# Modulation by column halves, later tables, and gate rows through DRAM, in a two-layer diffusion transformer block

## The reference

```python
sh1, sc1, gt1, sh2, sc2, gt2 = split(silu(cond) @ w_ada[l] + b_ada[l], 6)
h = rmsnorm(x, norm_mix_pre[l]) * (1 + sc1) + sh1
y = mixer(h)                      # w_in, four kinds of attention, w_o
x = x + gt1 * rmsnorm(y, norm_mix_post[l])
h = rmsnorm(x, norm_ffn_pre[l]) * (1 + sc2) + sh2
x = x + gt2 * rmsnorm(channel_mixer(h), norm_ffn_post[l])
```

## Time and profile before

| | us |
|---|---|
| median of three runs | 1594.75 (1592.17 to 1596.13) |
| the profiled execution | 1590.41 |
| its span on the core | 1588.2 |
| TensorE busy | 1516.3 (95%) |
| VectorE, ScalarE, GpSimd busy | 1166.0, 972.7, 116.3 |

### The profile page before, as it was taken

One profiled execution on the slowest core, in us unless ns is written; L12 is line 12 of the kernel. 1 busy time (PEld: TensorE's weight loads), 2 busy tenths in 40 slices (PEclk: granted clock), 3 DMA queues, 4 the chain that ended last, 5 costly groups with the idle time before them and its releaser, 6 DMA issues.

```text
span 1588.2 us, 22081 instructions
## 1 busy us (share of the span) xinstructions
PE 1516.3 (95%) x7825; PEld 1233.5 (78%) x7825; DVE 1166.0 (73%) x1001; ACT 972.7 (61%) x951; POOL 116.3 (7%) x167
## 2 busy tenths in 40 slices
PE   5989999999898999999999999999999999999996
PEld 2866799988676778878878887887887887887884
DVE  2568444535567548888888888888888888888886
ACT  3444444323544457777777777777777777777773
POOL 2430130000020110000000000000000000000001
PEclk9999999999998999999999999999999999999998
DMA  9966665567752379999999999999999999999991
GB/s 368 294 222 208 221 174 174 173 224 265 288 191 93 128 284 324 370 362 372 384 366 363 380 366 352 388 371 349 388 369 354 384 367 352 388 367 340 394 385 72
DMA packets 221317, 484.91 MB, mean 305 GB/s; under 512 B 8800, under 2 KB 41872, under 8 KB 221264
## 3 DMA queue, kind: packets, MB, share of 16 engines
q1 hardware_dynamic: 215024, 466.38, 81.3%
q0 software_dynamic: 6240, 17.80, 4.1%
HBM read 475.34 MB, written 8.81 MB: 305 GB/s over the span
## 4 chain that ended last, share of the span: by engine, by line
PE 89%; DVE 4%; ACT 3%; DMA 1%; issue 1%; POOL 1%; POOLq 0%; DVEq 0%; SPq 0%; ACTq 0%
PE ps L1700 23%; PE ps L1701 23%; PE ps L1705 23%; PE ps L1715 4%; PE ps L1722 3%; PE ps L1716 3%; PE ps L1745 2%; PE ps L2144 2%; DMA raw<-in_w_ada 1%; PE ps L1784 1%; PE ps L1923 1%; PE ps L1880 1%; ACT probs L851 1%; DVE sm L1283 1%; DVE qz L1247 1%
## 5 line engine op out<-in xcount | busy, mean ns | idle before, releaser
L1153 DVE TENSOR_TENSOR w_lo<-raw,w_hi 128x2048 fp32r<-128x2048 f32 (+1 forms) x397 | 905.6, 2285 | 204.1 <-ACT w_hi L771 201.5
L771 ACT ACTIVATE w_hi<-raw 128x2048 fp32r<-128x2048 f32 (+1 forms) x397 | 757.7, 1913 | 260.7 <-PE ps L1701 241.0
L1700 PE MATMUL ps<-w_hi,x_hi 128*128 128x512 f32 (+1 forms) x1216 | 436.1, 369 | 4.1 <-ACT w_hi L771 2.7
L1701 PE MATMUL ps<-w_hi,x_lo 128*128 128x512 f32 (+1 forms) x1216 | 430.9, 365 | 0.0
L1705 PE MATMUL ps<-w_lo,x_hi 128*128 128x512 f32 (+1 forms) x1216 | 285.9, 365 | 0.0
L1700 PEld LDWEIGHTS ps<-w_hi,x_hi 128*128 128x128 f32 x1216 | 229.0, 188 | 44.8 <-issue 5.2
L1701 PEld LDWEIGHTS ps<-w_hi,x_lo 128*128 128x128 f32 x1216 | 229.1, 188 | 38.0
L1705 PEld LDWEIGHTS ps<-w_lo,x_hi 128*128 128x128 f32 x1216 | 207.8, 188 | 39.9
L1700 PE MATMUL ps<-w_hi,h_hi 128*128 128x512 f32 x520 | 205.4, 395 | 4.9 <-DVE h_lo L1485 4.3
L1701 PE MATMUL ps<-w_hi,h_lo 128*128 128x512 f32 x520 | 205.4, 395 | 0.0
L1705 PE MATMUL ps<-w_lo,h_hi 128*128 128x512 f32 x520 | 139.0, 392 | 0.0
(11 more groups left out here) (265 smaller groups left out, 1074.2 us busy)
## 6 DMA issues: line engine op xcount, KB each, us to landing
raw<-in_moe_w_gate SPq DMA_DIRECT2D x112, 1024.0 KB, 6.4
raw<-in_moe_w_up SPq DMA_DIRECT2D x112, 1024.0 KB, 7.1
raw<-in_moe_w_down SPq DMA_DIRECT2D x112, 1024.0 KB, 6.7
raw<-in_w_ada SPq DMA_DIRECT2D x48, 1024.0 KB, 6.1
raw<-in_w_in SPq DMA_DIRECT2D x20, 960.0 KB, 11.0
raw<-in_ffn_w_gate SPq DMA_DIRECT2D x11, 1024.0 KB, 5.5
raw<-in_ffn_w_up SPq DMA_DIRECT2D x11, 1024.0 KB, 5.9
raw<-in_ffn_w_down SPq DMA_DIRECT2D x11, 1024.0 KB, 5.7
```

The lines of the kernel that those rows point to most:

```text
L771: act.activation(split_hi(c, slice(0, width(c))), raw[:, r % NRAW, 0:width(c)], ACT.Copy).then_inc(hi_done, 1)
L1153: dve.tensor_sub(split_lo(c, n), raw[:, raw_of(c) % NRAW, n], split_hi(c, n)).then_inc(lo_done, 1)
L1700: pe.matmul(out, xh, split_hi(c, w), start=start, stop=False, skip_group_check=True)
L1701: last = pe.matmul(out, xl, split_hi(c, w), start=False, stop=False, skip_group_check=True)
```

## The change

1. Scale and shift of layer 0 are made by column halves: units 4, 5, 0, 1 give columns 0 to 511 of both, units 6, 7, 2, 3 the rest. The stream has the first `w_in` contraction halves between them, and TensorE runs the first halves (h = 0) of blocks 0 to 2 for both sequences before the second halves. Between these first halves stand ada 6, 7 and 2, 3. The `w_in` blocks take six PSUM banks in turn instead of four. ScalarE keeps the second half of the transposes in `h` (`keep_T`).
2. The constants are reordered; the first load has 144 columns, the other 832 come by a second load ahead of the cache loads of layer 0, and these now start at the third `hi` instead of the second.
3. `gates` and `gate_rows` go. Once per layer and channel, TensorE transposes the gate columns of both sequences (`gate_cols`, two transposes), ScalarE copies them out, GpSimd stores them to DRAM (`gate_store`, 8 KB) and loads each sequence's row into all 128 partitions of `xn` (`gate_load`, 512 KB).

```diff
-            units += ada(0, 4, 5, 6, 7, 0, 1, 2, 3) + win + ada(0, 8, 9, 10, 11)
+            units += ada(0, 4, 5, 0, 1) + win[0:1] + ada(0, 6, 7) + win[2:3] + ada(0, 2, 3) + win[4:5] + win[1:6:2] + win[6:] + ada(0, 8, 9, 10, 11)
...
-ROW_BANK = {(0, 1): 7, (0, 0): 6, (1, 1): 1, (1, 0): 1}
+ROW_BANK = {(0, 1): 0, (0, 0): 0, (1, 1): 1, (1, 0): 1}
...
+def section_of(l, n):
+    if l == 0 and n < 8:
+        return (0, 1 - n // 2 % 2), 1 - n // 4, n in (4, 6), n in (1, 3)
+    return (l, n // 4), n // 2 % 2, n % 4 == 0, n % 4 == 3
...
-            return 4 * s if l or which else 2 * s
+            return 4 * s if l or which else 4 + 2 * s
...
-            src = ps[:, 2 + 2 * (j % 2) + s, :]
+            src = ps[:, 2 + 2 * (j % 3) + s, :]
...
-            pool.dma_start(cst[:, :], consts).then_inc(in_cst, 16)
+            pool.dma_start(cst[:, 0:C_FIRST], consts[:, 0:C_FIRST]).then_inc(in_cst, 16)
...
+            def gate_store(n):
+                pool.wait_ge(g_evac, n + 1)
+                pool.dma_start(g_dram[n].rearrange("s t c -> t s c"), g_cols[:, :, :]).then_inc(g_out, 16)
+                pool.wait_ge(g_out, 16 * (n + 1))
+            def gate_load(n, s):
+                if n % 2:
+                    pool.wait_ge(nT, 4 * n + 2 * s + 2)
+                else:
+                    pool.wait_ge(oT, n + s + 1)
+                pool.dma_start(xn[:, s, :], bass.AP(tensor=g_dram[n].tensor, offset=s * D, ap=[[0, P], [1, D]])).then_inc(g_in[s], 16)
...
-                    pool.wait_ge(hi_done, 2)
+                    pool.wait_ge(hi_done, 3)
+                    pool.dma_start(cst[:, C_FIRST:C_N], consts[:, C_FIRST:C_N]).then_inc(in_tables, 16)
...
+            def keep_T(s):
+                act.wait_ge(nT, 2 * s + 2)
+                act.activation(h_of(0, 0)[s][:, 512:1024], ps[:, T_bank(0, 0, s) + 1, :], ACT.Copy).then_inc(nkeep, 1)
...
+            def gate_cols(l, which, b):
+                n = 2 * l + which
+                act.wait_ge(g_T, n + 1)
+                if n:
+                    act.wait_ge(g_out, 16 * n)
+                act.activation(g_cols[:, :, :], ps[0:KT, b, 0:2 * P].rearrange("t (s c) -> t s c", s=2), ACT.Copy).then_inc(g_evac, 1)
...
                     rows(0, 1)
+                    split_to(1)
+                    for s in range(2):
+                        keep_T(s)
+                        norm_hi(0, 0, s, (0,))
+                    split_to(2)
                     rows(0, 0)
+                    split_to(4)
+                    act.wait_ge(nkeep, 2)
                     for s in range(2):
                         norm_h(0, 0, s)
-                        norm_hi(0, 0, s)
-                        split_to(s + 1)
+                        norm_hi(0, 0, s, (1,))
...
-                for n in range(2):
-                    gate_rows(l, 0, 0, n, n)
                 post_half(l, 0, 0)
...
-                dve.wait_ge(gbs, 2 * q + 2)
+                dve.wait_ge(g_in[s], 16 * (2 * l + which + 1))
...
                     section(0, 1)
...
+                        norm_h(0, 0, s)
+                        norm_lo(0, 0, s, (0,))
+                        split_to(s + 1)
+                    split_to(3)
                     section(0, 0)
+                    split_to(4)
                     for s in range(2):
+                        norm_lo(0, 0, s, (1,))
...
-            def gates(l, which, s, n, b):
+            def gate_cols(l, which, b):
                 k = 3 * which + 2
                 pe.wait_ge(mod_ready, SECTIONS.index((l, k)) + 1)
-                for i in range(4):
-                    last = pe.matmul(ps[:, b, cols(i, P)], mod[:, l, k, 4 * n + i, s:s + 1].to_broadcast([P, P]), ident(),
-                                     start=True, stop=True)
-                last.then_inc(gb, 1)
+                for s in range(2):
+                    last = pe.transpose(ps[0:KT, b, cols(s, P)], mod[:, l, k, :, s], ident())
+                last.then_inc(g_T, 1)
...
             def attention(l):
+                pe.wait_ge(win_evac[1], NWIN * l + 3)
...
+                    if i == 9:
+                        for s in range(2):
+                            pe.wait_ge(prep_evac[s], np_(s) * (l + 1))
+                        gate_cols(l, 0, 6)
                     item_out(l, i)
...
-                        if j == 0:
-                            if s:
-                                pe.wait_ge(gbs, 2 * (4 * l + 1))
-                            for n in range(2):
-                                gates(l, 0, s, n, n)
...
-                    if 1 <= f <= 4:
-                        pe.wait_ge(gbs, f + 3)
-                        gates(0, 1, (f - 1) // 2, (f - 1) % 2, 1)
+                    if f == 1:
+                        gate_cols(0, 1, 1)
...
-                for n in range(2):
-                    gates(1, 1, 0, n, 6 + n)
+                gate_cols(1, 1, 6)
...
-                pe.wait_ge(r_row, 1)
-                for n in range(2):
-                    gates(1, 1, 1, n, n)
...
+                if l == 0:
+                    for j in range(3):
+                        for s in range(2):
+                            w_in_unit(j, 0, s)
+                            for n in {(0, 1): (6, 7), (1, 0): (2, 3)}.get((j, s), ()):
+                                ada(0, n)
+                            if j == s == 1:
+                                columns(0, 0)
+                    for j in range(3):
+                        for s in range(2):
+                            w_in_unit(j, 1, s)
```

More of the change, by code:

```diff
@@ L191, in win_u, with win_c, half_count @@
     return SPLIT.index(("win", l, 0)) + 2 * j
+def win_c(l, j, h):
+    return SPLIT.index(("win", l, 2 * j + h))
+def half_count(q, h):
+    return 2 * h + q + 1 if q < 2 else 2 * q + h + 1
 def wo_u(l, j):
@@ L275, in program @@
         h_dram = nc.dram_tensor("h_rows", (2 * P, D), F32, kind="Internal").ap()
+        g_dram = [nc.dram_tensor(f"gate_rows{n}", (2, KT, P), F32, kind="Internal").ap() for n in range(2 * DEPTH)]
         y_dram = nc.dram_tensor("y_rows", (3 * P, D), F32, kind="Internal").ap()
@@ L822, in norm_h, with norm_hi @@
                     if q < 2:
-                        src, scale = h[:, P * k:P * k + P], 1.0
+                        src = h[:, P * k:P * k + P]
                     last = act.activation(h[:, P * k:P * k + P], src, ACT.Identity, bias=mod[:, l, 3 * which, k, s:s + 1], scale=scale)
                 last.then_inc(nh[1], 1)
-            def norm_hi(l, which, s):
+            def keep_T(s):
+                act.wait_ge(nT, 2 * s + 2)
+                act.activation(h_of(0, 0)[s][:, 512:1024], ps[:, T_bank(0, 0, s) + 1, :], ACT.Copy).then_inc(nkeep, 1)
+            def norm_hi(l, which, s, halves=(0, 1)):
                 q = 4 * l + 2 * which + s
-                for h in range(2):
+                for h in halves:
                     act.wait_ge(nh[h], q + 1)
@@ L1210, in norm_h, with norm_lo @@
                 last.then_inc(nh[0], 1)
-            def norm_lo(l, which, s):
+            def norm_lo(l, which, s, halves=(0, 1)):
                 q = 4 * l + 2 * which + s
-                for h in range(2):
+                for h in halves:
                     n = slice(512 * h, 512 * h + 512)
-                    dve.wait_ge(nhi, 2 * q + h + 1)
+                    dve.wait_ge(nhi, half_count(q, h))
                     dve.tensor_sub(x_lo[:, s, n], h_of(l, which)[s][:, n], x_hi[:, s, n]).then_inc(nlo, 1)
@@ L1734, in ada @@
             def ada(l, n):
-                r, h, m = AT["ada", l, n], n % 2, SECTIONS.index((l, n // 4))
-                if n % 4 == 0:
+                at, i, first, last_of = section_of(l, n)
+                r, h, m = AT["ada", l, n], n % 2, SECTIONS.index(at)
+                if first:
                     same = [i for i in range(m) if row_bank(i) == row_bank(m)]
@@ L1744, in ada @@
                 for kt in range(4):
[L1745 to L1746 removed]
+                    last = pe.matmul(row_ps(m)[CG * kt:CG * kt + CG, :], cond[:, 4 * h + kt, i, :],
+                                     raw[:, r % NRAW, 512 * kt:512 * kt + 512], start=first, stop=last_of)
                 last.then_inc(ada_used, 1)
```

128 lines of the change are left out of this document (66 added, 62 removed).

## The result

The changed kernel takes 1570.24 us in the median (1568.72 to 1572.64, four runs); the kernel before, timed beside it, 1595.44 (1592.17 to 1598.58). The ratio of the two is 0.9844, 95% interval 0.9819 to 0.9868. That is 25 us less, where 16.6 were forecast; it is 1.8 us under the low end of the range. The direction and the order of the work came as forecast. The size did not.

The account below looks back on a forecast made before the run. TensorE, with 89% of the chain of waits, was taken as the bound. Terms 4.9 + 7.3 + 3.3 + 1.1 = 16.6 us took 1590.41 to 1573.8; adding 4.3 for the timed median gave 1578, range 1572 to 1588.

Parts of the forecast that it names:

- four terms: Forecast gains: start of layer 0 4.9 us, out-projections 7.3, dense stage 3.3, before the experts 1.1; together 16.6.
- The start: Start of layer 0: four ada loads instead of eight ahead, attention's first ada at 87.2 us instead of 92.1, gain 4.9.
- the stall of a microsecond that the margins allowed: Start of layer 0: margins of 0.6 to 1 us for later operands, so a stall of about 1 us was possible.
- the 26.6: Start of layer 0: forecast time in us of the first w_in product, 10.1 us earlier than before.
- rival C: Start of layer 0 gains nothing, its halves adding hand-overs; total gain 11.7 us, 1583 us; chance 0.09.
- Gate rows: Out-projections and dense stage without gate-row products: forecast gains of 7.3 and 3.3 us.
- 9.8 us to go: Out-projections: time forecast for the gate-row load, from its issue at 157.4 us to gated() at about 167.2.
- Rival D: Out-projections: gate-row load lands late, 24 us in all, stalling each layer 14 us; about 1606 us; chance 0.05.
- Before the experts: Routing step without gate products: at most 2.3 us saved, term 1.1 us, bounds -1 and 2.3.
- The half of it that the text gave back to the clock: Before the experts: gather running wholly at half clock, giving back about 1.2 of at most 2.3 us.

Follow-up runs that it names:

- e2: The changed kernel with the constants' tile one column wider (977), so the tiles behind it lie as in the kernel before; 1579.11 us, ratio 0.9904.
- e16: The kernel before with the constants' tile at 1008 columns instead of 977; 1576.07 us.
- e9: The changed kernel with an 8-column gap ahead of its first tile, every tile 32 bytes further, distances kept; 1570.28 us, ratio 0.9855.
- e7: The changed kernel with the constants' tile at 992 columns instead of 976, everything behind it 64 bytes further; 1571.65 us.
- e3: The kernel before with the gate part of the change alone and the constants' tile at 992 columns; 1573.13 us, ratio 0.9866.
- e1: The kernel before with one edit, the constants' tile 992 columns wide instead of 977; 1584.80 us, ratio 0.9939.
- e4: The changed kernel with its gate part taken back, new start and 976-column constants' tile kept; 1581.22 us, ratio 0.9917.
- e5: The changed kernel with x_hi and x_lo (and the small tiles behind them) moved 32 bytes; 1580.13 us, ratio 0.9904.
- e15: The changed kernel with the constants' tile at 1104 columns, everything behind it 512 bytes further; 1570.95 us.
- e8: The changed kernel with 12 products nobody reads added in the routing step, where gate products were removed; 1570.74 us, ratio 0.9847.
- e14: The changed kernel with the constants' tile at 1040 columns, everything behind it 256 bytes further; 1572.31 us.
- e12: The changed kernel with the constants' tile at 1008 columns, everything behind it 128 bytes further; 1560.02 us.

## Why the prediction was wrong, point by point

**The step that failed** is the sum: "4.9 + 7.3 + 3.3 + 1.1 = 16.6 us. The profiled execution took 1590.41 us ... : 1573.8." It subtracts four terms and leaves every other product at its duration of before, a term put at nothing without a reason. The text read the new order of the constants as a matter of their transfer ("144 of 977 columns") and nowhere as a matter of where the tiles behind them lie. e2 shows the missing term: with the old distances the changed kernel takes 1579.1, 1.1 us from the forecast of 1578.0, and it is 15.4 us faster than the kernel before beside it, where 16.6 were forecast. The term that had to stand beside the four is the pace of some 6,000 products (three lines with 1216, 520 and 256 each), 8.9 us (e2 against the changed kernel), of which the profiles place 4.2 in the experts and 2.7 in the dense stage (184.6 us in e2, 182.0 after). The rest lies mostly in w_in and attention of layer 1 (125.8 us in e2, 123.2 after), where w_in products start 219 ns apart instead of 217 and e2's profile has 6.8 us more at half clock. That the four terms came out near in sum is in part luck: the parts below miss both ways.

**The start.** Right: 87.2 forecast for the first ada, 87.39 measured; sequence 1 at 32.27 (31.4), first product at 27.34 (26.6). The half clock there ended at 33.4 (33.5 forecast); the stall of a microsecond that the margins allowed didn't come. The parts listed for the 26.6 add up to 26.5.

What the start is worth in the end is less sure. In the profile after, attention of layer 0 takes 1.5 us more than before: a half-clock stretch (98.2 to 101.6) lies there, and the one of before (155.0 to 158.4) lay mostly in the out-projection, which helps to explain why that stage gained 5.0 and not 3.7. But this is not shown to be the work of the new start. e16, with the old start, has such a stretch and takes 64.9 us in attention; e9, with the new one, has it elsewhere and takes 63.5. With tiles at 992 columns the start was worth little: e7 is only 1.5 us faster than e3, though 4.9 ahead at the first ada (86.0 against 90.9); its profile has half clock in attention, around the norm of layer 0 and before the experts where e3's has full, and loses 1.4, 2.7 and 1.6 us there. There rival C (the start gains nothing) comes close to true. At the old distances and at 1008 columns the whole change is worth 15.4 and 16.1; if the gate part gives 11.7 there too, an estimate that no run checks, the start gives 3.7 and 4.4.

**Gate rows.** Right in sum: forecast 11.7, measured 11.7 (e1 to e3) and 11.0 (e4 to the changed kernel). The path of the load was wrong. The forecast let GpSimd issue it when the transposes were over, with 9.8 us to go, and gave the store no time. The store took 5.4 us in the median (6.0 in this stage), the load waited for it, and had 7.5 us (156.14 to 163.62). It took 7.3. That nothing stalled is luck by 0.2 us. Rival D, a landing later than 18 us, falls: the longest load took 9.3.

**Before the experts.** Forecast 1.1, measured -0.1. The half of it that the text gave back to the clock was too little: the gather ran at half clock for 3.7 us (the stretch of half clock ends at 572.7), where before it did so for 1.5, and took 5.4 us up to the first expert product instead of 4.3. In the 13 profiles of kernels without gate products or stand-ins (the changed one, e2, e3, e5 to e7, e9 to e15) half clock in this stage lasts 17.1 us nine times and 20.5 four times; in the four with gate products (before, e4, e1, e16) it lasts 6.8, 10.2, 13.7 and 13.7, and in e8 13.7. By the rule of the Trainium skill that the forecast weighed (TensorE: Matmul & The Clock Gate, "What's actually happening": activity is what releases the throttled state), the trace agrees, here and in e8.

**The half clock in sum.** To 640 us the profile of before has 34 us of it, that of after 51. Most of that difference is not the change's: e1 and e16, the kernel before with a wider tile, have 51 and 55, and e9, the changed kernel moved by 32 bytes, has 44. The granted clock of the timed executions says how much is left. It averages 0.9812 over 38 executions of the kernel before (0.977 to 0.986) and 0.9796 over 61 executions of kernels with gate rows from DRAM. Worked out from these, that is 60 and 64 us of half clock in the whole execution, an estimate, so that the change gives back some 2 us of time at most.

**What stays open.** Which mechanism makes a distance slow. That the accesses of the loaded and the streamed operand meet in the same part of the memory would fit, but no run looks into it. Why moving h changed products with x, and why the same products in the same tiles take two paces in one execution, is open as well; in the experts, work of ScalarE and VectorE on the same tiles may take part.

## What to carry to other kernels

Before you sum up the edits of a change, look whether any tile's size or place moved: on this kernel, bound by TensorE, that alone was worth 18 us of 1594 (e16), more than the whole written change. Compare two kernels at equal tile distances, and tune the distance by itself, over 256 bytes in steps of 32 or 64, for the shape that holds most of the time. When products are taken from a wait, count what they did for the clock of those behind; putting unread ones back gained no time here (e8). And compare sums of half clock over several executions, not over two profiles.

## What the runs showed of the hardware that was not expected

- At full clock, products of 512 columns start 227 to 235 ns apart in the mean, and of 256 columns 113 to 120, by how far apart in SBUF the loaded and the streamed tiles lie. A shift by 256 or 512 bytes changes nothing (e14, e15), nor does a common shift of all tiles by 32 (e9). The places aren't all that counts: the same products in the same tiles started 117.8 or 113.3 ns apart within one execution.
- It is exact: at equal distances the experts' stage took 983.7 us in two kernels (before, e2), 975.5 in three (e1, e3, e7), 967.1 in two (e12, e16) and 979.4 to 979.5 in six (the changed kernel, e4, e8, e9, e14, e15), although their other parts differ.
- An 8 KB store to DRAM landed after 5.4 us in the median of four (1.8 to 6.0).
